# Token and weight splits reordered at the start of the experts, and the last token tile in fused halves

## The reference

```
aff = softmax(h @ w_router)                        # 16 experts
gates, idx = top_k(aff.T, cap)                     # cap = 2*n/16: 128 prompt rows, 64 sample rows per expert
xe  = h[idx]
hid = silu(xe @ w_gate[e]) * (xe @ w_up[e])
out[idx] += (hid @ w_down[e]) * gates
x   = x + gt_f * out;   y = rms_norm(x, g_final)
```

## Time and profile before

| | before |
|---|---|
| median of 3 runs | 1526.52 us (1525.94 to 1529.21) |
| the profiled execution: time, span | 1527.16 us, 1525.4 us |
| PE busy | 1432.7 us (94%) |
| DVE, ACT, POOL busy | 1033.5, 774.9, 161.7 us |
| mean granted TensorE clock | 0.974 |
| DMA | 322.20 MB, mean 211 GB/s |

### The profile page before, as it was taken

The page is one execution under the profiler, slowest core; times in us unless marked ns, Lnnn a source line. Parts: engine busy times, 40 slices in busy tenths (PEclk is TensorE's granted clock), DMA queues, the critical chain, the costliest instruction groups (busy, mean ns, idle before and its releaser), DMA issues.

```text
span 1525.4 us, 22693 instructions
## 1 busy us (share of the span) xinstructions
PE 1432.7 (94%) x8583; PEld 1273.6 (83%) x8583; DVE 1033.5 (68%) x1445; ACT 774.9 (51%) x1016; POOL 161.7 (11%) x128
## 2 busy tenths in 40 slices
PE   2999999999999983999999999999999999999992
PEld 1787777887787862999999999999999999999992
DVE  3421533677769776777777777777777777767776
ACT  4422121523542323666666666656666666666564
POOL 2000000000000001020121021021021122022020
PEclk9999999999999995999999999999999999999996
DMA  9233344555331364687787788788788788778786
GB/s 325 103 119 125 117 147 151 192 170 180 101 106 56 131 226 154 193 265 247 247 271 236 248 267 245 249 270 242 254 258 247 259 251 244 272 244 266 253 276 241
DMA packets 217941, 322.20 MB, mean 211 GB/s; under 512 B 7452, under 2 KB 174440, under 8 KB 217896
## 3 DMA queue, kind: packets, MB, share of 16 engines
q1 hardware_dynamic: 208760, 294.70, 58.4%
q0 software_dynamic: 8064, 26.30, 7.4%
q10 hardware_dynamic: 1072, 0.59, 0.1%
HBM read 290.07 MB, written 31.49 MB: 211 GB/s over the span
## 4 chain that ended last, share of the span: by engine, by line
PE 85%; DVE 7%; ACT 3%; DMA 2%; SPq 1%; issue 1%; POOL 0%; POOLq 0%; DVEq 0%; ACTq 0%
PE ps L1183 26%; PE ps L1505 25%; PE ps L1503 10%; PE ps L1518 4%; PE ps L1526 4%; PE ps L1527 4%; PE ps L1519 4%; PE ps L1522 4%; PE ps L1508 1%; DVE wlo L2044 1%; SPq L610 1%; PE ps L1494 1%; ACT whi L1089 1%; DMA ada_w<-in_w_ada 1%; PE ps L1294 1%
## 5 line engine op out<-in xcount | busy, mean ns | idle before, releaser
L1505 PE MATMUL ps<-xT,whi 128*128 128x384 f32 x2048 | 576.9, 357 | 4.9 <-DVE xT L2050 4.9
L2044 DVE TENSOR_TENSOR wlo<-raw,whi 128x2048 fp32r<-128x2048 f32 x192 | 437.4, 2292 | 191.9 <-ACT whi L1089 191.9
L1503 PE MATMUL ps<-xT,wlo 128*128 128x192 f32 x1792 | 455.4, 254 | 0.0
L1505 PEld LDWEIGHTS ps<-xT,whi 128*128 128x128 f32 x2048 | 368.1, 189 | 5.8 <-issue 5.3
L1089 ACT ACTIVATE whi<-raw 128x2048 fp32r<-128x2048 f32 x192 | 362.3, 1906 | 0.0
L1503 PEld LDWEIGHTS ps<-xT,wlo 128*128 128x128 f32 x1792 | 342.7, 191 | 0.0
L1183 PE MATMUL ps<-hT,wring 128*128 128x512 f32 x1224 | 290.1, 396 | 5.8 <-DVE hT L1636 5.8
L1183 PEld LDWEIGHTS ps<-hT,wring 128*128 128x128 f32 x1224 | 229.7, 190 | 58.8 <-DVE hT L1636 6.2
L1119 ACT ACTIVATE gu_l<-ps 128x384 f32<-128x384 f32 x128 | 62.9, 491 | 160.5 <-PE ps L1505 160.5
L1183 PE MATMUL ps<-wo,Yhl 128*128 128x512 f32 x576 | 135.3, 393 | 1.3 <-ACT h2T L1013 1.0
L1183 PEld LDWEIGHTS ps<-wo,Yhl 128*128 128x128 f32 x576 | 107.0, 188 | 24.0 <-ACT h2T L1013 1.4
(11 more groups left out here) (214 smaller groups left out, 1546.1 us busy)
## 6 DMA issues: line engine op xcount, KB each, us to landing
raw<-in_w_gate SPq DMA_DIRECT2D x64, 1024.0 KB, 5.0
raw<-in_w_up SPq DMA_DIRECT2D x64, 1024.0 KB
raw<-in_w_down SPq DMA_DIRECT2D x64, 1024.0 KB, 5.3
wraw<-in_w_in SPq DMA_DIRECT2D x34, 512.0 KB, 6.0
wraw<-in_w_ada SPq DMA_DIRECT2D x32, 512.0 KB, 4.9
ada_w<-in_w_ada SPq DMA_DIRECT2D x16, 512.0 KB, 11.2
acc_d<-x SPq DMA_DIRECT2D x12, 512.0 KB, 2.7
h_d<-h SPq DMA_DIRECT2D x12, 512.0 KB, 4.2
```

Of the source, the lines that this page charges most:

```text
L1503: pe.matmul(out[:, 0:CAP], wlo[:, slot, w], xT[:, k, 0:CAP], start=False, stop=False, skip_group_check=True)
L1505: mm = pe.matmul(out[:, 0:2 * CAP], whi[:, slot, w], xT[:, k, :], start=k == 0, stop=k == KB - 1, skip_group_check=True)
L2044: dve.tensor_tensor(wlo[:, j % SPL, :], raw[:, j % RAW, :], whi[:, j % SPL, :].bitcast(F32), ALU.subtract).then_inc(w_split, 1)
```

## The change

1. `ROUNDS`: one round of top eight is taken from step 10 and one from step 11, and one is added at step 17 and one at step 20.
2. The last tile of the sample (`last_tile` on VectorE, `last_squares` on ScalarE): VectorE drains all three groups itself, in halves of 512 columns, each multiplied by its norm and by gt_m at once, and adds them up; the scaling by gsf starts before the root is there. ScalarE squares the halves apart. TensorE issues the logits of tile 1 and the transposes of tile 2 ahead of the last group of w_out instead of behind it, and ScalarE drains both halves of h2T for the tiles 1 and 2.
3. The start of the experts: GpSimd makes the low part of chunk 0. TensorE transposes the prompt rows right behind the affinities, ahead of the index columns, and the sample rows later, into a bank of their own. ScalarE splits chunks 0 and 1, then the tokens, then chunks 2 and 3; VectorE chunk 1, the tokens, then chunks 2 and 3.

```diff
-ROUNDS = {9: 1, 10: 2, 11: 2, 12: 2, 14: 2, 15: 2, 16: 2, 17: 1, 19: 1, 20: 1}
+ROUNDS = {9: 1, 10: 1, 11: 1, 12: 2, 14: 2, 15: 2, 16: 2, 17: 2, 19: 1, 20: 2}
...
+    if name == "h2T" and key[1] and key[2] in (TL[1] - 3, TL[1] - 2):
+        return "act"
...
@@ gpsimd
             pool.nop().then_inc(ye_free, 1)
+            pool.wait_ge(w_hi, 1)
+            pool.tensor_tensor(wlo[:, 0, :], raw[:, 0, :], whi[:, 0, :].bitcast(F32), ALU.subtract).then_inc(w_split, 1)
             pool.wait_ge(first_rows, 1)
...
@@ scalar
+            def last_squares():
+                tt = NT - 1
+                for n, ready in enumerate((x2_first, x2_ready)):
+                    cols = slice(GW * n, GW * (n + 1))
+                    act.wait_ge(ready, 1 if n == 0 else NT)
+                    act.activation(xr[:, tt % 2, cols], x2[:, tt % 2, cols], ACT.Square, accum_out=ssh[:, n:n + 1]
+                                   ).then_inc(half_sum, 1)
+                    if n == 0:
+                        act.wait_ge(half_sum, 1)
+                        act.activation(ss2[:, tt:tt + 1], ssh[:, 0:1], ACT.Identity, bias=eps[:, :], scale=1.0 / D
+                                       ).then_inc(ss2_ready, 1)
+                act.wait_ge(half_sum, 2)
+                act.wait_ge(ss2_ready, NT)
+                act.activation(rs2[:, tt:tt + 1], ssh[:, 1:2], ACT.Sqrt, bias=ss2[:, tt:tt + 1], scale=1.0 / D
+                               ).then_inc(std_2, 1)
...
-            for i in range(4):
+            for i in range(2):
                 split(0, i)
-            tokens_hi(0)
+            first_tokens_hi()
+            for i in range(2, 4):
+                split(0, i)
...
@@ vector
+            def last_tile():
+                s, t, tt = 1, TL[1] - 1, NT - 1
+                x, h, r = x2[:, tt % 2, :], h2[:, tt % GT, :], rs2[:, tt:tt + 1]
...
+                for k in NORMS:
+                    to = x if k == NORMS[0] else h
+                    for n, cols in enumerate(half):
+                        wait_filled(dve, "out", s, t, k, n)
+                        drain(dve.scalar_tensor_tensor(out=to[:, cols], in0=bank("out", s, t, k, n),
+                                                       scalar=rsy[:, tt, k:k + 1], in1=gtm_b[:, cols], op0=ALU.mult,
+                                                       op1=ALU.mult), "out", s, t, k, n)
+                    for n, cols in enumerate(half):
+                        wait_drained(dve, "out", s, t, k, n)
+                        ins = dve.tensor_tensor(x[:, cols], x[:, cols], (xr[:, tt % 2, :] if k == NORMS[0] else h)[:, cols],
+                                                ALU.add)
...
             dve.memset(tick[:, 0:1], 0.0).then_inc(ye_sum, 1)
-            for i in range(4):
-                split(0, i)
-            tokens_lo(0)
+            dve.wait_ge(w_split, 1)
+            split(0, 1)
+            for k in range(4):
+                first_tokens_lo(k)
+            dve.wait_ge(t_hi, 4)
+            dve.tensor_tensor(xT[:, :, CAP + CAP_P:2 * CAP], sample_of(range(KB)), xT[:, :, CAP_P:CAP].bitcast(F32),
+                              ALU.subtract).then_inc(t_lo, 4)
+            for i in range(2, 4):
+                split(0, i)
```

More of the change, by code:

```diff
@@ L202, in bank_events @@
             for k in NORMS:
+                if s and t == TL[1] - 1 and k == NORMS[2]:
+                    job("lg", 1, t - 2)
+                    router_blocks(1, t - 1)
                 for h in range(2):
@@ L228, in bank_events @@
         job("aff", 1, g)
+    for k in range(GT + 1):
+        opened("xe", k)
     job("idx", 1)
@@ L261, in bank_plan @@
             now_open.discard(home[key])
+        elif key[0] == "xe":
+            home[key], before[key] = key[1], user.get(key[1])
+            user[key[1]] = key
+            now_open.add(key[1])
         elif key in ADA_HALF:
@@ L408, in encoder_kernel @@
     smax = small("smax", [TL[0], 1])
+    ssh = small("ssh", [2])
     tick = small("tick", [2])
@@ L556, in encoder_kernel, with first_of, sample_of @@
     w_d = a["w_down"][0].rearrange("e (k p) f -> e p k f", p=P)
+    def first_of(k, first, end):
+        return ps[:, k, 0:2 * CAP].rearrange("p (a n) -> p a n", a=2)[:, :, first:end]
+    def sample_of(blocks):
+        return bank("xe", GT).rearrange("p (k n) -> p k n", k=KB)[:, blocks.start:blocks.stop:blocks.step, :]
     def load_chunk(eng, e, j):
@@ L1010, in h2T_drain @@
             def h2T_drain(s, t):
[L1011 to L1014, removed]
+                for half in range(2):
+                    if drainer["h2T", s, t, half] != "act":
+                        continue
+                    wait_filled(act, "h2T", s, t, half)
+                    wait_h2t_free(act, s, t)
+                    drain(act.activation(h2T[:, GT * half:GT * (half + 1), :].rearrange("p b n -> p (b n)"),
+                                         bank("h2T", s, t, half), ACT.Copy), "h2T", s, t, half)
+            def last_squares():
[13 more added lines that the diff above has]
+                               ).then_inc(std_2, 1)
             def lg_drain(s, t):
@@ L1027, in residual @@
                         h2T_drain(s, t - 2)
-                    for h in range(2):
+                    for h in range(2) if tt < NT - 1 else ():
                         wait_filled(act, "out", s, t, NORMS[0], h)
@@ L1484, in _, with first_tokens, sample_tokens @@
             affinity_rows(1)
+            def first_tokens():
+                for k in range(4):
+                    open_bank("xe", k)
+                    pe.wait_ge(xe_in, 16)
+                    for i in range(2):
+                        cols = slice(P * (k + 4 * i), P * (k + 4 * i + 1))
+                        tr = pe.transpose(ps[:, k, CAP * i:CAP * i + CAP_P], xe[:, 0, cols], ident[:, :])
+                    tr.then_inc(prompt_in, 1)
+            def sample_tokens():
+                pe.wait_ge(xe_in, 32)
+                for k in range(4):
+                    pe.transpose(sample_of(range(k, k + 5, 4)), xe[:, 1, P * k:P * (k + 1)], ident[:, :]).then_inc(t_filled, 1)
+                pe.wait_ge(prompt_lo, 4)
+            first_tokens()
+            open_bank("xe", GT)
             index_columns(1)
@@ L1812, in h2T_drain @@
             def h2T_drain(s, t):
+                if drainer["h2T", s, t, 1] != "dve":
+                    return
                 wait_filled(dve, "h2T", s, t, 1)
@@ L1866, in residual @@
                     after_step()
[L1867 to L1874, removed]
+                    hh = h2[:, tt % GT, :]
+                    step(dve.scalar_tensor_tensor(out=hh, in0=x2[:, tt % 2, :], scalar=r, in1=gsf_b[:, :], op0=ALU.mult,
+                                                  op1=ALU.mult))
+                    after_step()
+                    dve.tensor_tensor(hh, hh, shf_b[:, :], ALU.add).then_inc(h2_ready, 1)
                     if s == 0 and t == GT + 1:
```

67 lines of the change are left out of this document (50 added, 17 removed).

## The result

| | before | changed |
|---|---|---|
| median, timed side by side | 1526.7 us (1525.9 to 1529.2, 4 runs) | 1517.66 us (1516.89 to 1518.71, 4 runs) |
| profiled execution: time, span | 1527.16, 1525.4 us | 1517.95, 1516.1 us |
| mean granted TensorE clock | 0.974 | 0.976 |

The ratio is 0.9941, 95% interval 0.9925 to 0.9957: faster by 9.0 us of the medians, where 7.7 were forecast. A second set of runs (experiment 10) gave 0.9939 (0.9926 to 0.9953). Forecast and range held; one of the three terms was too small, because a cost was missing in it.

The account below looks back on a forecast made before the run. TensorE was taken to bound the kernel where busy, VectorE's steps the stretch before the experts, besides TensorE's wait for v and the last tile; -1.8 - 0.8 - 5.1 = -7.7 us, median 1518.8 us, range 1515.8 to 1523.3.

Parts of the forecast that it names:

- Part 1: Moved rounds, gating to first w_out product: wait for v goes (-2.5), wait for Y's low parts comes (+0.7), -1.8 us.
- TensorE had arrived 2.5 us before 459.9: Before the gating: TensorE was ready at 457.4 and waited for v until 459.9.
- The whole 2.5 us goes at that place: Before the gating: v can end near 456.8, so TensorE's wait of 2.5 us vanishes.
- Part 2: Last tile of the sample: second transposes of h2 start at 569.36 instead of 570.16, -0.8 us.
- Part 3: Start of the experts: first expert product at 597.6 instead of 602.68, -5.1 us.
- The first: Rival: moved rounds and last tile bring nothing, only the experts' -5.1 us stays, 1521.4 us; chance 0.14.
- The second: Rival: in the routing, GpSimd's split and the top eights exclude each other, costing 5.8 us, 1524.6 us; chance 0.12.
- The fourth: Rival: GpSimd's split waits until the routing ends, near 591.2, delaying the gather; 1533.6 us if 15 us long; chance 0.04.
- The third: Rival: more gained at the gating wait, last tile and experts' clock, -10.6 us in all, 1515.9 us; chance 0.10.
- higher clock back a microsecond sooner: First expert: TensorE pauses 1.5 us and not 5 before its first product, worth -1.0 us.

Follow-up runs that it names:

- experiment 10: The changed kernel itself, run again beside the kernel with a better placed round and three fill-ins: 1517.87 us.
- experiment 1: Kernel before with only the two moved top-eight rounds: 1525.49 us, ratio 0.9983.
- experiment 3: Kernel before, rounds unmoved, with 10 unread matmuls keeping TensorE busy while it waits for v: 1526.58 us, ratio 0.9993.
- experiment 4: Changed kernel with the low part of chunk 0 made by VectorE again instead of GpSimd: 1518.92 us, ratio 0.9939.
- experiment 6: Changed kernel with the start of the experts as it was before, moved rounds and last tile kept: 1523.71 us, ratio 0.9976.
- experiment 8: Changed kernel with unread matmuls before the last h2 transposes (13), before the sample rows' transposes (9) and behind those (3): 1516.28 us, ratio 0.9926.
- experiment 9: Changed kernel with one round moved from step 20 to the sample's w_out tile 0, plus unread matmuls (13, 9, 3) in TensorE's waits: 1513.04 us, ratio 0.9912.
- experiment 11: Experiment 9's kernel plus 10 unread matmuls in TensorE's wait for the sample's first hT near 393 us: 1512.17 us, ratio 0.9892.

## Why the prediction was right, and where it was short

**Part 1, forecast -1.8, measured -2.9: the term that was mis-sized.** What was to happen did happen. v's four products end at 456.95 (forecast 456.8), the wait is gone, and the low parts of Y are late instead, by 0.99 us (0.7 forecast). The step that fell short is the one from "TensorE had arrived 2.5 us before 459.9" to "The whole 2.5 us goes at that place": it priced the wait at its own length. Its real price was 2.47 + 1.67 us, as the clock was halved behind it; experiments 1 and 3 show it from both sides. Of the 4.1 us, the wait for Y takes back 0.99 and TensorE's change-over from the DFT 0.25. The trace of before had it: 48 gating matmuls in 4.51 us, and a granted clock of 0.98, not 1.00, in the stage from 460 to 561. I had read that 0.98 as nothing.

**Part 2, forecast -0.8, measured -1.05.** The last w_out product ends at 560.24, the inverse is there (564.34) 4.1 us later (forecast 4.3), and the second four of the eight transposes, which begin near 566.2, stand 6.0 us behind it (forecast 6.2).

**Part 3, forecast -5.1, measured -4.9.** From the gather's issue to the first product 6.29 us (forecast 6.15): landing after 3.58, transposes 1.09, high part 0.60, low part 0.69. GpSimd's split takes 4.52 us, not the 5.8 taken, begins 2.0 us after ScalarE's first one and is done at 577.1, 10 us ahead of VectorE's need. The 4497 ns of the Trainium skill (GPSIMD Engine Reference, Elementwise — side-by-side cycle accounting) agree with these 4.52 us. TensorE waits for nothing at f = 2. Little of the term is GpSimd's, though: without its split only 0.5 us is lost (experiment 4), and the rest comes from the order of the splits and tokens.

**The rivals.** The first (rounds and last tile bring nothing) is out by experiment 1 (2.9 us for the rounds) and by the ledger's 1.05 us for the last tile, which experiment 6 bears out within its noise. The second (GpSimd excludes the top eights) is out: 10.89 us for the rounds against 10.90, and 10.90 beside three subtractions. The fourth (GpSimd kept out until the routing ends) is out: it started when its input was there. The third pointed the right way. Its "higher clock back a microsecond sooner" is worth little in the first expert: the clock is at 0.5 for 3.4 us there and was for 4.2, which is 0.4 us of time and not 1.0. The clock that mattered was at the gating.

## What to carry to other kernels

Price a wait of TensorE by what stands behind it too: compare the same matmuls there with their rate elsewhere and read the granted clock of the next microseconds. Where the wait can't be removed, products that nobody reads can fill it; four such places and one round better placed brought by the ratios another 0.5% here, some 7 us (0.9892 against 0.9939). Work moved off a late engine should be moved only as far as its wait goes: up to the first w_out product one round brought 3.8 us, two 2.9.

## What was not expected of the hardware

Behind waits of 2.20, 2.35 and 2.47 us of a TensorE that had been busy, the granted clock was 0.5 (its lower level, 1.2 GHz); behind waits of 0.32 and 0.99 us it was not. Behind the 2.47 us it was at 0.5 for 3.5 us of dense matmuls before it rose.

The length of a wait does not settle it alone. In the changed kernel's last tile, where TensorE's work had been thin from 561 on, the clock fell at 563.0, 1.2 us after the last product; in experiment 8 it fell at 578.0, 3.4 us after the last one, and it had come back at 574.6 behind 12 small transposes. Sparse work can cost the clock as well: it fell at 571.1 in experiment 8, where no single wait from 559 on had been over 1.9 us. In experiment 9's kernel the same work, from 559 to 570, kept it at 1.00; in experiment 11's, with the same instructions there, it fell at 571.5. What decides between them stays open.

VectorE's eight rounds ran beside a 13.67 us chain of GpSimd at full rate, while a copy of 16x64 took 2.07 us instead of 0.18.
